# A split-float32 matmul tile, reordered from row by row to three passes, each pass waiting only for its own parts

## The reference, cut to what matters

```python
def swiglu(x, w_in, w_out):
    a, gate = jnp.split(x @ w_in, 2, axis=-1)
    return (jax.nn.silu(a) * gate) @ w_out
...
x = layer_norm(ALPHA * x + 0.5 * swiglu(x, w['ffn_w_in'][l, 0], w['ffn_w_out'][l, 0]), g[0], b[0])
if l < N_A:  y, hr, hi = s5_mixer(...)        # ends in z @ w_glu
else:        y = diff_attention(...)          # x @ w_q, shared_kv: x @ w_kv, ... @ w_o
x = layer_norm(ALPHA * x + y, g[1], b[1])
x = layer_norm(ALPHA * x + 0.5 * swiglu(x, w['ffn_w_in'][l, 1], w['ffn_w_out'][l, 1]), g[2], b[2])
```

## Time and profile before

| | |
|---|---|
| median of three runs | 2349.99 us (2346.33 to 2350.52) |
| profiled execution, its own time | 2352.45 us |
| its span, first to last instruction | 2350.6 us |
| mean granted TensorE clock | 0.987 of full speed |
| PE / PEld / DVE / ACT / POOL busy | 96% / 94% / 65% / 49% / 25% |
| the three matmul lines | 14976 of 17067 matmuls |

### The profile page before, as it was taken

One profiled execution on the slowest core, in us unless ns is written; L12 is line 12 of the kernel. 1 busy time (PEld: TensorE's weight loads), 2 busy tenths in 40 slices (PEclk: granted clock), 3 DMA queues, 4 the chain that ended last, 5 costly groups with the idle time before them and its releaser, 6 DMA issues. The chain is left out here.

```text
span 2350.6 us, 42458 instructions
## 1 busy us (share of the span) xinstructions
PE 2257.9 (96%) x17067; PEld 2215.2 (94%) x17067; DVE 1519.6 (65%) x2284; ACT 1155.4 (49%) x1947; POOL 581.1 (25%) x499
## 2 busy tenths in 40 slices
PE   8999999999998998999999999999999999899997
PEld 8989999999998998999999999999999998889997
DVE  6888768656788677444474575655677665465444
ACT  4445543555644556433355465655466554354332
POOL 3256401123210253111251123011352011142110
PEclk9999999999999999999999999999999999999999
DMA  9567676454665455555569655544556456355552
GB/s 249 167 185 225 183 217 187 123 170 135 201 214 169 126 168 149 183 149 149 147 187 288 187 159 172 153 122 138 146 156 189 134 150 185 108 146 162 145 155 79
DMA packets 702292, 391.11 MB, mean 166 GB/s; under 512 B 25001, under 2 KB 689042, under 8 KB 702098
## 3 DMA queue, kind: packets, MB, share of 16 engines
q1 hardware_dynamic: 662720, 332.44, 49.3%
q10 hardware_dynamic: 39378, 55.96, 7.0%
HBM read 366.53 MB, written 21.82 MB: 165 GB/s over the span
## 5 line engine op out<-in xcount | busy, mean ns | idle before, releaser
L473 DVE TENSOR_TENSOR wl<-raw,wh 128x1024 fp32r<-128x1024 f32 (+1 forms) x640 | 795.2, 1243 | 469.0 <-ACT wh L467 467.2
L489 PE MATMUL tile_ps<-xh,wh 128*128 128x256 f32 (+1 forms) x3520 | 1056.8, 300 | 29.1 <-DVE wl L473 16.4
L490 PE MATMUL tile_ps<-xl,wh 128*128 128x256 f32 (+1 forms) x3520 | 1038.6, 295 | 0.0
L491 PE MATMUL tile_ps<-xh,wl 128*128 128x256 f32 (+1 forms) x3520 | 1038.2, 295 | 0.0
L467 ACT CAST wh<-raw 128x1024 fp32r<-128x1024 f32 (+1 forms) x640 | 655.4, 1025 | 753.0 <-PE tile_ps L491 743.7
L489 PEld LDWEIGHTS tile_ps<-xh,wh 128*128 128x128 f32 x3520 | 668.6, 190 | 39.1 <-DVE wl L473 21.0
L490 PEld LDWEIGHTS tile_ps<-xl,wh 128*128 128x128 f32 x3520 | 668.4, 190 | 1.0 <-issue 0.2
L491 PEld LDWEIGHTS tile_ps<-xh,wl 128*128 128x128 f32 x3520 | 668.5, 190 | 0.0
L605 POOL TENSOR_TENSOR hl<-hf,hh 128x256 fp32r<-128x256 f32 (+1 forms) x176 | 247.9, 1408 | 1285.4 <-ACT hh L531 1284.8
L489 PE MATMUL tile_ps<-hh,wh 128*128 128x320 f32 (+1 forms) x1472 | 444.0, 302 | 12.8 <-POOL hl L605 10.2
L490 PE MATMUL tile_ps<-hl,wh 128*128 128x320 f32 (+1 forms) x1472 | 433.7, 295 | 0.0
(11 more groups left out here) (295 smaller groups left out, 1773.9 us busy)
## 6 DMA issues: line engine op xcount, KB each, us to landing
raw<-in_ffn_w_in_dram SPq DMA_DIRECT2D x352, 512.0 KB, 3.8
raw<-in_ffn_w_out_dram SPq DMA_DIRECT2D x128, 448.0 KB, 3.6
raw<-in_ffn_w_out_dram SPq DMA_DIRECT2D x64, 512.0 KB, 3.9
raw<-in_ssm_w_glu_dram SPq DMA_DIRECT2D x32, 512.0 KB, 3.8
raw<-in_attn_w_kv_dram SPq DMA_DIRECT2D x32, 512.0 KB, 3.9
wt<-scr_w ACTq DMA_DIRECT2D x16, 512.0 KB, 4.2
cp<-scr_c ACTq DMA_DIRECT2D x16, 512.0 KB, 4.1
raw<-in_attn_w_q_dram SPq DMA_DIRECT2D x16, 512.0 KB, 3.7
```

The lines of the kernel that those rows point to most:

```text
L473: nc.vector.tensor_tensor(wl[n % WS][:, 0:k, :], raw[n % RAWS][:, 0:k, :], wh[n % WS][:, 0:k, :].bitcast(F32), ALU.subtract).then_inc(w_lo, 1)
L489: nc.tensor.matmul(o, wh[w][:, kk, :], xa, start=kk == 0, stop=False)
L490: nc.tensor.matmul(o, wh[w][:, kk, :], xb, start=False, stop=False)
L491: mm = nc.tensor.matmul(o, wl[w][:, kk, :], xa, start=False, stop=kk == ROWS[n] - 1)
```

## The change

A tile's matmuls go in three passes over its rows: all high by high, then low weights by high x, then high weights by low x. PE waits for the high weights (`w_hi`) ahead of the first pass and for the low weights (`w_lo`) ahead of the second. In a first tile the first pass waits row by row for the high part of x, and the third row by row for the low part. The matmuls are the same in number and shape.

```diff
-        def pe_tile(pe, n, h, hi, lo, ready=None, have=0):
+        def pe_tile(pe, n, h, hi, lo, high_ready=None, low_ready=None, have=0):
+
+            pe.wait_ge(w_hi, n + 1)
+            wait(pe, drained[n % PSS], n // PSS)
+            o, w, count = ps[:, n % PSS, 0:NT[h]], n % WS, ROWS[n]
+            for kk in range(count):
+                if high_ready is not None:
+                    pe.wait_ge(high_ready, have + kk + 1)
+                nc.tensor.matmul(o, wh[w][:, kk, :], hi[:, kk, 0:NT[h]], start=kk == 0, stop=False)
             pe.wait_ge(w_lo, n + 1)
-            wait(pe, drained[n % PSS], n // PSS)
-            o, w = ps[:, n % PSS, 0:NT[h]], n % WS
-            for kk in range(ROWS[n]):
-                if ready is not None:
-                    pe.wait_ge(ready, have + kk + 1)
-                xa, xb = hi[:, kk, 0:NT[h]], lo[:, kk, 0:NT[h]]
-                nc.tensor.matmul(o, wh[w][:, kk, :], xa, start=kk == 0, stop=False)
-                nc.tensor.matmul(o, wh[w][:, kk, :], xb, start=False, stop=False)
-                mm = nc.tensor.matmul(o, wl[w][:, kk, :], xa, start=False, stop=kk == ROWS[n] - 1)
+            for kk in range(count):
+                nc.tensor.matmul(o, wl[w][:, kk, :], hi[:, kk, 0:NT[h]], start=False, stop=False)
+            for kk in range(count):
+                if low_ready is not None:
+                    pe.wait_ge(low_ready, have + kk + 1)
+                mm = nc.tensor.matmul(o, wh[w][:, kk, :], lo[:, kk, 0:NT[h]], start=False, stop=kk == count - 1)
             mm.then_inc(tile_done, 1)
...
-                pe_tile(pe, FIRST["out", f, h, p] + d, h, hh, hl, None if d else hl_ready, HID[f, h, p])
+                n = FIRST["out", f, h, p] + d
+                if d:
+                    pe_tile(pe, n, h, hh, hl)
+                else:
+                    pe_tile(pe, n, h, hh, hl, hh_ready, hl_ready, HID[f, h, p])
```

More of the change, by code:

```diff
@@ L501, in pe_plain @@
             for i in range(count):
-                pe_tile(pe, FIRST[key] + i, h, high, low, None if i else x_ready[h], have)
+                if i:
+                    pe_tile(pe, FIRST[key] + i, h, high, low)
+                else:
+                    pe_tile(pe, FIRST[key], h, high, low, xh_ready[h], x_ready[h], have)
                 step(beside)
@@ L506, in pe_in @@
             for i in range(2 * PARTS[p]):
-                pe_tile(pe, FIRST["in", f, h, p] + i, h, xh[h], xl[h], None if i or p else x_ready[h], X_OF_FFN[f])
+                n = FIRST["in", f, h, p] + i
+                if i or p:
+                    pe_tile(pe, n, h, xh[h], xl[h])
+                else:
+                    pe_tile(pe, n, h, xh[h], xl[h], xh_ready[h], x_ready[h], X_OF_FFN[f])
                 step(beside)
```

## The result

The changed kernel takes 2359.49 us (median of 20 runs, 2349.94 to 2365.66), the kernel before 2351.20 in 20 runs beside it: ratio 1.0033, 95% interval 1.0023 to 1.0044. It is slower by 0.33%, above the 0.2% that was called the bound. The forecast of 2350.4 with "no change" as the likeliest outcome was 9 us too low; the time lies inside the range, near its upper end. The profiled execution of the changed kernel took 2360.26 us (span 2357.4, mean granted clock of TensorE 0.984) against 2352.45 (2350.6, 0.987).

The account below looks back on a forecast made before the run. PE, busy 96% of the span, was taken to bound the kernel through matmul steps and its waits. Terms +4.0 - 2.7 - 0.9 = +0.4 us gave 2350.4 us, with an 8-in-10 range of 2339 to 2361.

Parts of the forecast that it names:

- no change: Whole kernel: time stays within about 0.2%, 4.7 us, of the kernel before; chance 0.52.
- the rival in which the fast tiles of 256 columns turn slow: Matmul steps at 256 columns: all 134 fast tiles go to the slow level, +14 us, 2365; chance 0.24.
- the other way: Matmul steps at 256 columns: the 181 slow tiles go to the fast level, -19 us, 2332; chance 0.09.
- Matmuls and satisfied waits, 0: All tiles: the 14976 matmuls and their weight loads stay, and a third wait costs nothing when met; 0 us.
- The rule on the reuse of weights: Skill's rule that loaded weights serve several matmuls: by it passes would add 4992 loads; by the profile rows, none.
- First tiles of the "out" stages, +4.0: First tiles on hidden values: pass one wants the last `hh` earlier, so twelve of 24 stages pay; +4.0 us in all.
- First tiles on x, -2.7: First tiles on x: low parts come last, so one step instead of three follows the last `xl`; -2.7 us.
- Late low weights, -0.9: Tiles with late `wl` end sooner, but later waits take the gain back except at 1223.18; -0.9 us.
- of the same kind as rows 6: ("in", 0, 0, 0), ("in", 1, 0, 0) and ("in", 3, 0, 0), likened to ("in", 3, 1, 0): gains of 0.4, 0.5 and 0.3 us.
- the clock as a rival: First tiles, where the granted clock is 0.50 for 10.2 us: 5 us could be won, 2345; chance 0.05.
- the +0.4 of the sum: Whole kernel: +4.0 for "out" first tiles, -2.7 for first tiles on x, -0.9 for late low weights.

Follow-up runs that it names:

- the order alone: Kernel before with later tiles in three passes behind the one wait for low weights in front, first tiles as before: ratio 0.9997.
- changed kernel with fillers: Changed kernel plus 42 useless identity products, put into the next tile's bank before five of PE's waits: 2350.66 us, ratio 0.9994 to the kernel before.
- the row order: Kernel before, still row by row, but in first tiles high and low parts each have their own wait: 2346.91 us, ratio 0.9979; with fillers at nine places 2340.38.
- fillers at nine places: Row by row with own waits in first tiles, plus useless products before nine of PE's waits: 2340.38 us, ratio 0.9940 to the kernel before.

## Why the prediction was right or wrong, step by step

The time lies in the stated range, but the forecast of "no change" didn't come, and the kernel lost its time by a mechanism that no rival had. The range reached that far up for the rival in which the fast tiles of 256 columns turn slow (2365). That didn't happen: by the median step of each tile, 155 are now at the fast level and 155 at the slow one, where the prediction counted 134 and 181; by its own price of 24 x 0.0045 us a tile that is a gain of about 2 us. (Its sum for the other way has 23 for 24, 0.8 us too little, and nothing hangs on it.) So it is luck that the range holds the time.

**Matmuls and satisfied waits, 0: right.** The steps are unchanged and the order alone gave 0.9997 (0.9986 to 1.0008). The rule on the reuse of weights changed nothing: there are 17067 weight loads again.

**First tiles of the "out" stages, +4.0: right in the tiles.** The run with passes there alone fits it (+2.3 us by the ratio, interval 0 to 4.7) but can't tell it from 1 or 2 us. The rows that answer to the earlier trace rows:

```profile
1007.27 1.19 PE L489 MATMUL tile_ps<-hh,wh 128*128 128x320 f32 x7
...
1008.47 0.45 ACT L547 CAST hh<-hf 128x320 fp32r<-128x320 f32 x1
...
1008.98 0.41 PE L489 MATMUL tile_ps<-hh,wh 128*128 128x320 f32 x1 [0.52 <-ACT hh L547]
1009.00 1.56 POOL L621 TENSOR_TENSOR hl<-hf,hh 128x320 fp32r<-128x320 f32 x1 [5.47 <-ACT hh L547]
1009.23 1.34 PE L492 MATMUL tile_ps<-hh,wl 128*128 128x320 f32 x8
```

PE stands for 0.52 us for the last `hh`, then runs through, and this tile falls back by 0.42 us for the 0.43 of the prediction. The other terms, from the starts of the last matmuls: 0.79 at ("out", 0, 1, 0) for 0.8, 0.42 at ("out", 3, 1, 0) for 0.43, and 0.26 at each of the six with K = 7 and 320 columns. Where PE had stood long before the tile, the clock enters: ("out", 1, 0, 0) lost 1.46 for 0.56, and ("out", 1, 0, 1) 1.75 for a gain of 0.1, of which 0.9 and 1.0 came back later in the same stages.

**First tiles on x, -2.7: four of the terms right, one of the wrong sign.** ("o", 1) gained 0.66 (0.7), ("in", 1, 0, 0) 0.38 (0.5), ("in", 3, 0, 0) 0.20 (0.3), ("in", 3, 1, 0) 0.58 (0.7). The last is to be read against the earlier trace rows:

```profile
2102.08 2.33 PE L492 MATMUL tile_ps<-xh,wl 128*128 128x320 f32 x8
2102.39 3.34 POOL L771 TENSOR_TENSOR xl<-r,xh 128x320 fp32r<-128x320 f32 x4
2104.22 1.99 PE L496 MATMUL tile_ps<-xl,wh 128*128 128x320 f32 x8
```

Pass two runs at half clock (8 in 2.33 us), and pass three starts at 2104.22 without a wait on `xl`. But ("in", 0, 0, 0) lost 1.24 where I had put a gain of 0.4:

```profile
11.68 2.09 PE L489 MATMUL tile_ps<-xh,wh 128*128 128x256 f32 x6 [1.30 <-ACT xh L957]
13.57 1.91 PE L492 MATMUL tile_ps<-xh,wl 128*128 128x256 f32 x8
15.28 1.75 PE L496 MATMUL tile_ps<-xl,wh 128*128 128x256 f32 x8
```

Pass one ends with the last `xh`, as in an "out" stage, and all sixteen products behind it run at half clock (8 in 1.91 us; at full clock 1.07), while the order of before had done part of them by then. Of the 1.24 us, 0.53 are left at the end of the stage. That it was "of the same kind as rows 6" was taken over, not worked out.

**Late low weights, -0.9: the waits moved as said; what moving them costs was missed.** From 748 to 778 us the wait moved along: with the earlier trace rows beside it, DVE's idle time is 1.9 us again, the groups from 751 to 786 us have 5.8 us of PE's wait on `wl` and a new one of 2.4 on ACT's `wh` (for 9.1 and none), and the stall at L1598 grew:

```profile
L473 DVE TENSOR_TENSOR wl<-raw,wh 128x1024 fp32r<-128x1024 f32 x9 | 11.7, 1296 | 1.9 <-ACT wh L467 1.8
...
L492 PE MATMUL tile_ps<-xh,wl 128*128 128x256 f32 x56 | 8.7, 300 | 5.8 <-DVE wl L473 5.8
...
782.90 0.45 PE L1598 MATMUL misc<-u,tt 128*128 128x80 f32 x2 [1.32 <-DVE hs L1414]
```

At the earlier trace rows the wait before L1715 fell from 0.99 to 0.29 us:

```profile
950.91 1.09 PE L1715 MATMUL misc<-ident,kT 128*128 128x128 f32 x8 [0.29 <-DVE kT L1689]
```

PE came there later by 0.7 us, set against the kernel before, than it had begun the `k` stage, since two passes ahead of it ran at half clock (8 in 1.89 us, at 941.70 and 943.38). In ("in", 2, 0, 0) the 0.9 came out as 0.90 in the changed kernel with fillers and as 0.4 without.

**The step that failed** is in the same part: "Each tile ends 0.94 us sooner and waits 0.94 us more for the next `wl`, and after the last PE waits for `hs`, from DVE again (779.97). The gain is 0." A microsecond moved from one wait into another was priced at nothing. The part on lengths held, but a long wait is more often followed by half clock than a short one. In the changed kernel's trace the place at 440.83 shows it: the earlier waits got shorter, the last one longer (1.44 to 2.60), and behind it the clock was granted at half. In the runs the changed kernel loses 4 to 6 us more to the clock than the kernel before, and fillers in front of five waits take some 9 us off it, 4 off the kernel before.

The prediction had the clock as a rival, but in the first tiles alone and only for its gain. The Trainium skill (TensorE: Matmul & The Clock Gate, HAM oscillation), that gaps between bursts bring the low clock back, was cited there for a faster kernel because the waits would be fewer. They are as many (the waits on `hh` are 16, for 11 on `hl`), and elsewhere some are longer. The page's own example has waits that are longer than the bursts between them; that waits of 1.4 to 2.6 us on an engine 96% busy can be followed by half clock is what the traces here show.

**What stays open.** The cost in the rest (1.5 to 2.4 us, for the +0.4 of the sum) is 1.1 to 2.0 us above the sum. The misjudged ("in", 0, 0, 0), 0.53 lost for 0.4 gained at the end of its stage, can be 0.9 of it, and the scatter is 1. Why PE was granted full clock behind the 2.15 us wait at 1201 us before and not after, when the waits are the same, no run tells. Why some stages changed the level of their step (("out", 2, 0, 2) and ("q", 0) to the fast one, 0.7 us gained each) is open too; it doesn't decide the time.

## What to carry to other kernels

On an engine that is 96% busy a wait has two prices: its length, and the clock behind it. A change that moves idle time from several short waits into one long one can't be put down as neutral: look what the granted clock does behind the waits that grow, and in several executions, since the same wait is followed by either clock. For operands that come late, the order that gained here (0.9979) is the one that asks for each as late as it is needed (the high row at its own turn, the low product last in its row); the one that asks for all of one kind first lost (1.0033). Where a long wait can't be removed, try products into a bank that is overwritten next, fewer than fill the wait: 42 of them were worth 4 us in the kernel before and some 9 in the changed one, 78 again some 9 in the row order.

## What the runs showed of the hardware

- The granted clock fell behind a wait of PE of 1.6 us in starts (at 441 us, with 24 products of 64 columns right behind the wait), and behind one and the same wait it fell in one trace and not in another (`zq` near 1201 us, 2.15 us, three of seven traces). Over seven traces it fell with 6 of 139 waits under 1 us, 17 of 85 of 1 to 2 us and 52 of 77 of over 2 us. Over the runs of one kernel the time goes with the mean clock: in the changed kernel's 20 the correlation is -0.81, and the two of about 2350 us are those at 0.987 and 0.988.
- With fillers at nine places the mean clock was 0.990 to 0.993 and five runs lay within 1.1 us; without any, 28 runs of the kernel before had 0.984 to 0.988 and spread over 10.6 us (2348.20 to 2358.80).
